# 23 of the 26 gate-weight low parts of GpSimd go to VectorE, between the steps of the branches

## The reference, cut to what matters

```python
proj = h @ w_in
y_a = short_conv_mixer(...)          # a 3-tap convolution
y_b = stick_breaking_attention(...)  # 4 heads
y_c = rwkv7_mixer(...)               # a linear recurrence, in chunks of 64 tokens
y_d = spatial_gating(...)            # layer norm, then a causal 128x128 mix
gates = sigmoid(proj[..., GATE_OFF:] + gate_b)   # 4 branches x 1024 columns
merged = sum of gates[:, :, i] * (y_i @ out_i) over the four branches
return merged @ w_o
```

## Time and profile before

| | us |
|---|---|
| median of 3 runs | 1601.89 (1600.25 to 1605.63) |
| the profiled execution, its own time | 1597.99 |
| its span in the profile | 1596.2 |
| TensorE busy | 1569.5 (98%) |
| VectorE busy | 1193.2 (75%) |
| ScalarE busy | 817.6 (51%) |
| GpSimd busy | 429.5 (27%) |

### The profile page before, as it was taken

How to read it: one execution, slowest core, us unless ns; L and a number is a source line. 1 busy time by engine, 2 the same in 40 slices (tenths; PEclk the granted TensorE clock), 3 DMA queues, 4 the chain that set the end, 5 groups by cost and what they waited for, 6 DMA issues and landing times. The chain is left out here.

```text
span 1596.2 us, 33679 instructions
## 1 busy us (share of the span) xinstructions
PE 1569.5 (98%) x11762; PEld 1445.3 (91%) x11762; DVE 1193.2 (75%) x2303; ACT 817.6 (51%) x1350; POOL 429.5 (27%) x252
## 2 busy tenths in 40 slices
PE   9999999999999999999999999999999999999997
PEld 8998988999999877899999999999999888888886
DVE  7895157887886877356899998778775777777776
ACT  6573345655644742344544445555555555555554
POOL 0615510454420013576779960000000000000000
PEclk9999999999999999999999999999999999999998
DMA  8433443566655221355468885555667777777773
GB/s 313 148 109 117 121 172 121 186 185 186 188 178 187 74 70 44 132 195 162 146 208 232 233 230 178 178 172 179 178 178 234 251 242 235 233 241 230 241 234 116
DMA packets 93100, 289.56 MB, mean 181 GB/s; under 512 B 10336, under 2 KB 27104, under 8 KB 92768
## 3 DMA queue, kind: packets, MB, share of 16 engines
q1 hardware_dynamic: 92736, 287.81, 57.8%
q10 hardware_dynamic: 288, 0.71, 0.2%
HBM read 270.65 MB, written 17.83 MB: 181 GB/s over the span
## 5 line engine op out<-in xcount | busy, mean ns | idle before, releaser
L265 PE MATMUL psum<-arena_parts,ring_parts 128*128 128x256 f32 (+1 forms) x1856 | 522.0, 281 | 0.0
L263 PE MATMUL psum<-arena_parts 128*128 128x256 f32 (+1 forms) x1632 | 468.5, 287 | 6.4 <-DVE arena_parts L1640 2.6
L2825 DVE TENSOR_TENSOR ring_parts<-ring,arena_parts 128x512 fp32r<-128x512 f32 x414 | 280.2, 691 | 156.0 <-ACT arena_parts L2624 93.1
L265 PEld LDWEIGHTS psum<-arena_parts,ring_parts 128*128 128x128 f32 x1856 | 352.6, 190 | 0.0
L263 PEld LDWEIGHTS psum<-arena_parts 128*128 128x128 f32 x1632 | 307.9, 189 | 8.4 <-issue 4.5
L264 PE MATMUL psum<-h_parts,arena_parts 128*128 128x256 f32 x1024 | 286.1, 279 | 0.0
L258 POOL TENSOR_TENSOR ring_parts<-ring,arena_parts 128x1024 fp32r<-128x1024 f32 x81 | 214.9, 2679 | 62.0 <-ACT arena_parts L254 46.6
L2592 PE MATMUL psum<-arena_parts,x_parts 128*128 128x512 f32 x512 | 201.3, 393 | 0.3 <-DVE x_parts L2861 0.3
L2593 PE MATMUL psum<-ring_parts,x_parts 128*128 128x512 f32 x512 | 201.5, 394 | 0.0
L2594 PE MATMUL psum<-arena_parts,x_parts 128*128 128x512 f32 x512 | 201.2, 393 | 0.0
L264 PEld LDWEIGHTS psum<-h_parts,arena_parts 128*128 128x128 f32 x1024 | 193.5, 189 | 0.0
(11 more groups left out here) (556 smaller groups left out, 3178.8 us busy)
## 6 DMA issues: line engine op xcount, KB each, us to landing
ring<-stream SPq DMA_DIRECT2D x473, 512.0 KB, 3.7
kept<-arena SPq DMA_DIRECT2D x128, 128.0 KB, 2.2
arena<-kept SPq DMA_DIRECT2D x32, 512.0 KB, 4.7
arena<-first SPq DMA_DIRECT2D x1, 2144.0 KB, 17.0
arena<-second SPq DMA_DIRECT2D x1, 1632.0 KB, 6.9
out<-arena SPq DMA_DIRECT2D x4, 256.0 KB, 2.1
x<-x_t SPq DMA_DIRECT2D x2, 256.0 KB, 4.7
x<-x_t SPq DMA_DIRECT2D x1, 512.0 KB, 6.1
```

The source lines that it names most:

```text
L263: nc.tensor.matmul(dst, stationary[0], moving[0], start=first, stop=False)
L265: return nc.tensor.matmul(dst, stationary[1], moving[0], start=False, stop=last_one)
L2825: v.tensor_tensor(low[:, s, w], ring[:, s, w], expert_high[:, m % 2, w].bitcast(F32), ALU.subtract)\
```

## The change

`VECTOR_LOWS` becomes 3 to 31. GpSimd makes the low parts of gates 0 to 2 only, and then has nothing to do until the end of the stage. VectorE makes the other 29, in its own list, at places written out by hand. Nothing else changes: no transfer, no product, no work of ScalarE.

```diff
-        VECTOR_LOWS = range(3, 9)
+        VECTOR_LOWS = range(3, 32)
...
                 vec.link(v.tensor_reduce(mean, v_sg, AX, ALU.add))
+                gate_low(dve, v, 9)
                 vec.link(v.tensor_scalar(mean, mean, 1.0 / T, None, ALU.mult))
...
                     vec.link(v.tensor_scalar(sg_d[:, tt, :], v_sg[:, tt, :], mean[:, tt:tt + 1], None, ALU.subtract))
+                gate_low(dve, v, 10)
                 vec.link(v.tensor_tensor(sg_q, sg_d, sg_d, ALU.mult))
...
+                gate_low(dve, v, 11)
                 dve.wait_ge(S("sb_exp"), 1)
...
                 vec.tell(v.tensor_tensor(halves[1][0], halves[1][0], halves[1][1], ALU.mult), S("sb_weights"))
+                gate_low(dve, v, 12)
                 dve.wait_ge(S("sg_mixed"), 1)
...
                     vec.tell(v.tensor_tensor(by_half(dst), pairs_of(b, half), each(f(m)), ALU.mult), S("pair_read"), 4 + kind)
+                for n in (13, 14, 15):
+                    gate_low(dve, v, n)
                 for lev in range(2, LEVELS + 1):
                     dve.wait_ge(S("level_z"), lev - 1)
                     vec.tell(v.tensor_tensor(NT, MT, eight(lv[:, lev, :]), ALU.mult), S("level_nt"), lev)
+                    gate_low(dve, v, 12 + 2 * lev)
                     grow(dve, v, lev - 1)
+                    gate_low(dve, v, 13 + 2 * lev)
                 grow(dve, v, LEVELS)
+                gate_low(dve, v, 24)
...
                 vec.tell(v.tensor_copy(AM[:, :, 64:P], b3(2, 64)), S("mv_read"))
+                for n in (25, 26, 27):
+                    gate_low(dve, v, n)
...
                 vec.tell(v.tensor_tensor(y0[:, :, 64:T], y0[:, :, 64:T], b3(3)[:, :, 64:T], ALU.add), S("rw_y"))
+                gate_low(dve, v, 28)
...
                 vec.tell(v.tensor_tensor(yd2, y0, y0, ALU.mult), S("gn_squares"))
+                gate_low(dve, v, 29)
...
                 vec.tell(v.reciprocal(yd2, yd2), S("gn_inverse"))
+                for n in (30, 31):
+                    gate_low(dve, v, n)
                 dve.wait_ge(S("gn_root"), 1)
```

## The result

The changed kernel takes 1610.25 us (median of 7 runs, 1606.52 to 1615.59) against 1600.37 us of the kernel before (7 runs, 1597.12 to 1605.63). The ratio is 1.0064, with a 95% interval of 1.005 to 1.0079: slower by 0.64%. The sum had +10.2 us, measured are +9.9 us. The forecast of 1612 us is 1.75 us too high mainly because it was put on the median of three runs of before (1601.89 us); over seven runs that median is 1.5 us lower.

The account below looks back on a forecast made before the run. TensorE, busy 98%, was taken as the bound, so only its waits and lower clock count. +5.45 us (B, with A in it) and +4.8 us (C) gave +10.2 us on the 1601.9 us median: 1612 us, range 1606.5 to 1616.5.

Parts of the forecast that it names:

- The sum: Whole stage: +5.45 us up to gate 13, gain at the norm included, and +4.8 us at the group norm: +10.2 us.
- Place A: Spatial gate's norm: VectorE steps shed 4.06 us, two low parts add 2.3 us, wait and clock dip shrink: -3.45 us.
- Gates 11 and 12: Behind L724 and the attention weights: low parts ready several us before TensorE comes, so cost nothing.
- the levels: Five levels, gates 14 to 24: two low parts each, 2.4 us, covered by VectorE's waits; cost 0.
- gates 24 to 27: Gates to 24 hide in the levels, 25 to 27 in VectorE's 13.6 us wait for the chunk operators; cost 0.
- Place B: Gate 13 after the pair products: TensorE waits 6.6 us, half clock 2.3 us; +5.45 us with the norm's gain included.
- Place C: Group norm: 0.2 to 0.3 us at gate 28, 2.8 us wait at gate 30, dip 1.7 us: +4.8 us.
- the rule I took from three rows: TensorE's clock: an idle of 2.3 us or more costs 1.7 us on top, one of 1.75 us or less nothing.
- rival 1: Waits at gates 13 and 30 come but the clock doesn't fall: +6.25 us, 1608 us; chance 0.12.
- the second: Clock stays low longer behind gate 13, into the first level, and at group norm: +13.8 us, 1616 us; chance 0.14.
- the third: Faster: freed VectorE steps gain 4.55 us and no low part is late: 1597 us; chance 0.04.

Follow-up runs that it names:

- Run alone: The kernel before with only the low parts of gates 9 and 10 given to VectorE, GpSimd keeping 11 to 31: 1596.03 us, ratio 0.9979.
- the four instructions without purpose: The changed kernel plus four 128x512 GpSimd subtractions nobody reads, after the high parts of gates 9 and 10: 1617.87 us, ratio 1.0111.
- The filled wait: The changed kernel plus six 128x512 float32 products, later written over, ahead of TensorE's wait at gate 13: 1607.02 us, ratio 1.0045.
- my first repair: The changed kernel with gate 13's low part moved ahead of the pair products' reads: 1607.09 us, ratio 1.0049.
- the best order: The changed kernel with the low parts of gates 13, 14, 28 and 30 moved earlier into VectorE's idle stretches: 1596.85 us, ratio 0.9983.

## Why the prediction was right, point by point

**Place A: right in mechanism and size.** L711 and L713 shed 1.97 and 2.10 us, the wait is 0.5 us (0.6 predicted), no half clock behind it. In the run with gate 13's low part moved, gate 13 starts 3.46 us earlier than before (134.92 against 138.38 us). Run alone it gives 3.4 us (3.45 predicted), and the four instructions without purpose show that the cause is GpSimd's access to SBUF and not the traffic of the low parts.

**Gates 11 and 12, the levels, gates 24 to 27: right.** In the changed kernel there are three waits for L355 in all, at gates 13, 28 and 30. Of the two idles of VectorE that were to shrink, the one for the chunk operators does (13.6 to 5.6 us); the four at L580 do not in total (12.2 and 12.3 us).

**Place B: right, the clock a little over-sized.** 6.64 us of wait for 6.6 us, gate 13 starts at 141.77 us for 141.55 us, L743's counterpart L747 takes 0.69 us as predicted (the nine steps end at 140.36 us for 140.2 us), and the clock costs 1.8 us for 2.3 us (4.8 us for gate 13 against 3.0 us). The whole place is +5.2 us for +5.45 us. The filled wait shows that this part is the clock and is due to the idle.

**Place C: the waits right, the step on the clock wrong.** 0.23 us at gate 28 (0.2 to 0.3 predicted) and 2.70 us at gate 30 (2.8 predicted). The step that failed is the rule I took from three rows: "an idle of 2.3 us or more costs 1.7 us on top, one of 1.75 us or less nothing". One profile of the changed kernel has a stretch of half clock behind idles of 0.28, 0.79, 0.73 and 0.23 us around gate 28 and none behind 2.70 us, the other none around gate 28 and one behind 2.70 us. The 2.6 us at L1640, one of the three rows, have no fall behind them in five of the ten profiles; and 1.78 us, hardly more than the third row's 1.75 us, have one in the changed kernel's second profile. The sum held because in each profile of the changed kernel exactly one such stretch falls into the end of the stage. That number is not fixed by the waits: with the same idles around gate 28 and the same 2.70 us, the filled wait has no stretch there and the run with gate 13's low part moved has two. So it was luck as far as the prediction goes.

A smaller slip is hidden in gate 28. I had TensorE ready for it at 212.2 us in the old trace, but its first product starts at 211.79 us there, 0.57 us behind L954's start at 211.22 us. In the changed kernel it starts 1.36 us behind L969's (217.69 and 216.33 us): it is 0.8 us later, not 0.23 us, since the row gives the idle only.

**The sum.** -3.45 (A) + 6.64 + 1.8 (B) + 0.23 + 2.70 + 1.7 (C and one half-clock stretch) = +9.6 us, and the output products start 9.9 us later. By the starts of the products alone, B is +5.2 us and C is +4.7 us (4.8 predicted): 0.8 us for gate 28's later start, 1.1 us for half clock in it, 2.9 us at gate 30, less 0.1 us elsewhere. The lower end of the range, 1606.5 us, does not follow as told: rival 1's 1608 us less half a us is 1607.5 us. It doesn't matter here.

**What I had not seen.** The low part of gate 14 was late too, by 2.54 us, hidden behind gate 13's. It changes nothing in the forecast, but together with the clock it made my first repair gain about 3 us instead of 8.9 us.

The rivals: the clock fell (against the first), and did not stay low into the levels (against the second); the third, faster, needs the low parts of gates 13, 14 and 30 in time, and the best order, where they are, is faster than before by 0.17%.

## What to carry to other kernels

Work that is moved to an in-order engine is priced by its place, not by its length: TensorE waits for none of 23 instructions of 1.22 us in the best order, and the kernel is 10 us slower than before in the tried one, all through the few that stood behind steps which themselves waited for TensorE. For each one write down when its consumer comes to it, with the lateness in front taken away, since a late one hides the next. And take two short instructions off GpSimd where VectorE's chain is on the path before moving twenty-three: that had the whole gain (0.21%, against 0.17% with all 23 in the best order).

## What was not expected of the hardware

TensorE's clock falls from 2.4 to 1.2 GHz at different places in two executions of one program with equal waits: at 217 to 221 us in one, at 227 to 231 us in the other. Counted over the ten profiles of this case, from the windows and TensorE's timelines:

| TensorE's idle | its length, us | profiles with half clock right behind it |
|---|---|---|
| at gate 13 | 6.63 to 6.64 | 4 of 4 |
| for `sg_normed` (GpSimd kept busy; the kernel before) | 4.68 and 2.33 | 2 of 2 |
| at gate 14 | 2.54 | 2 of 2 |
| at gate 30 | 2.70 to 2.71 | 3 of 5 |
| at L1640 | 2.59 to 2.60 | 5 of 10 |
| at the place of 815 us | 1.78 to 2.42 | 4 of 4 |
| the same place | 1.41 to 1.75 | 0 of 6 |
| group norm, several close together | 0.79 and 0.73, most with 0.2 to 0.3 more | 4 of 10 |

Behind the long waits, at gate 13 and for 4.68 us, the clock was low before TensorE started again. Most stretches cost up to 1.7 us (busy time times one less the clock). By the starts of the products it is 1.8 us at gate 13, 1.1 us at gate 28 and 1.5 us at gate 30; behind gate 30 in the run with gate 13's low part moved, where half clock lasted twice as long, it is 2.8 us (9.10 us from gate 30's first product to the output products, against 6.35 us at full clock). No length of a single idle tells: between 2.3 and 2.7 us, 13 of 20 have a fall behind them, and idles of 0.8 us and less close together have one too. So a forecast should give such a stretch a chance and not a certainty, and a difference of 1.7 us between two single profiles can be this alone. And more work was faster: six products without purpose in a wait of 6.64 us took 1.8 us off the products behind it.
